# Expert layer: the gathered tokens of a round, from eight column blocks fetched by index and transposed instead of four

## The reference, cut to what matters

```python
e_flat = idx.reshape(-1)                      # 384 tokens x 8 experts
order = jnp.argsort(e_flat)                   # assignments sorted by expert, padded to blocks
x_pad = jnp.concatenate([xt, jnp.zeros((1, D), xt.dtype)], axis=0)
def block(args):
    rows, e = args
    xb = x_pad[rows]                          # the gather
    return (jax.nn.silu(xb @ w1[e]) * (xb @ w3[e])) @ w2[e]
out = lax.map(block, (row_token.reshape(n_blocks, MOE_BLOCK), block_expert)).reshape(R, D)
return jax.ops.segment_sum(out * row_gate[:, None], row_token, num_segments=T + 1)[:T]
```

## Time and profile before

| what | value |
|---|---|
| median of 3 runs | 1431.32 us (1430.42 to 1434.19) |
| the profiled execution's own time | 1430.79 us |
| its span, first to last instruction | 1428.9 us |
| mean granted TensorE clock | 0.994 |
| TensorE products busy | 1392.2 us, 97% of the span, 8025 instructions |
| VectorE, ScalarE, GpSimd busy | 39%, 30%, 21% |
| DMA | 319.70 MB, 223 GB/s read and written in HBM over the span |
| queue 1 (sync) | 307.25 MB in 98416 packets |
| queue 0 (GpSimd's indirect DMAs) | 8.39 MB in 2560 packets |

### The profile page before, as it was taken

How to read it: one execution, slowest core, us unless ns; L and a number is a source line. 1 busy time by engine, 2 the same in 40 slices (tenths; PEclk the granted TensorE clock), 3 DMA queues, 4 the chain that set the end, 5 groups by cost and what they waited for, 6 DMA issues and landing times.

```text
span 1428.9 us, 21288 instructions
## 1 busy us (share of the span) xinstructions
PE 1392.2 (97%) x8025; PEld 984.6 (69%) x8025; DVE 556.2 (39%) x1136; ACT 430.5 (30%) x1021; POOL 306.9 (21%) x247
## 2 busy tenths in 40 slices
PE   7999999999999999999999998999999999999996
PEld 2695898889888986888988865445544455444552
DVE  3467342885356576433222383111212112221124
ACT  3232212222644362223320422222232223222223
POOL 0430323324055542554141010000000000000001
PEclk9999999999999999999999999999999999999998
DMA  9540423213202539321135344999999999999991
GB/s 370 183 134 6 136 81 118 89 60 118 92 27 89 163 143 351 112 89 60 37 126 171 133 192 176 417 418 417 404 400 407 401 397 400 403 403 400 400 385 45
DMA packets 107379, 319.70 MB, mean 224 GB/s; under 512 B 9777, under 2 KB 69937, under 8 KB 78769
## 3 DMA queue, kind: packets, MB, share of 16 engines
q1 hardware_dynamic: 98416, 307.25, 56.0%
q0 software_dynamic: 2560, 8.39, 1.8%
q10 hardware_dynamic: 6336, 3.15, 0.8%
HBM read 314.83 MB, written 3.93 MB: 223 GB/s over the span
## 4 chain that ended last, share of the span: by engine, by line
PE 94%; DMA 2%; DVE 2%; ACT 1%; issue 0%; POOL 0%; SPq 0%; POOLq 0%; DVEq 0%
PE banks L629 21%; PE banks L596 19%; PE banks L2892 16%; PE banks L2941 8%; PE banks L2801 7%; PE banks L1036 4%; PE banks L2779 4%; PE banks L1182 1%; PE banks L868 1%; DMA ring<-in_ada_w 1%; PE banks L603 1%; PE banks L680 1%; PE banks L748 1%; PE banks L2787 1%; PE banks L2793 1%; PE banks L1241 1%
## 5 line engine op out<-in xcount | busy, mean ns | idle before, releaser
L2892 PE MATMUL banks<-w,xg 128*64 128x512 f32 (+1 forms) x1312 | 235.1, 597 | 0.0
L2892 PEld LDWEIGHTS banks<-w,xg 128*64 128x64 f32 (+1 forms) x1312 | 73.8, 127 | 154.5 <-issue 135.5
L3233 POOL DMA_INDIRECT fetched<-token_rows,row_of_place x32 | 30.4, 951 | 503.5 <-DVE row_of_place L3194 456.5
L629 PE MATMUL banks<-hT,ring 128*128 128x192 f32 x792 | 137.7, 326 | 0.0
L629 PEld LDWEIGHTS banks<-hT,ring 128*128 128x128 f32 x792 | 129.7, 190 | 2.1 <-DMA ring<-in_w_in 0.5
L2941 PE MATMUL banks<-w,hidT 128*64 128x512 f32 (+1 forms) x656 | 123.9, 600 | 0.3 <-ACT hidT L2985 0.3
L2801 PE MATMUL banks<-y,selT 128*128 128x512 f32 x384 | 110.7, 410 | 0.0
L629 PE MATMUL banks<-x,ring 128*128 128x192 f32 x528 | 96.9, 327 | 0.9 <-ACT late L1358 0.9
L629 PE MATMUL banks<-x,combos 128*128 128x192 f32 x528 | 96.6, 326 | 0.0
L3075 DVE SCALAR_TENSOR_TENSOR hid<-banks,gslot,sil 128x256 f32<-128x256 f32 x33 | 15.9, 483 | 201.8 <-ACT sil L2983 191.9
L2801 PEld LDWEIGHTS banks<-y,selT 128*128 128x128 f32 x384 | 66.1, 189 | 35.3 <-issue 26.2
(11 more groups left out here) (484 smaller groups left out, 2058.3 us busy)
## 6 DMA issues: line engine op xcount, KB each, us to landing
w<-in_exp_w SPq DMA_DIRECT2D x198, 1024.0 KB, 10.5
ring<-in_w_in SPq DMA_DIRECT2D x46, 1024.0 KB, 5.3
ring<-in_ada_w SPq DMA_DIRECT2D x24, 1024.0 KB, 7.3
ring<-in_w_branch SPq DMA_DIRECT2D x8, 1024.0 KB, 6.1
ring<-in_w_out SPq DMA_DIRECT2D x4, 1024.0 KB, 6.1
arena<-in_sh_w SPq DMA_DIRECT2D x3, 1024.0 KB, 8.0
x<-in_x_sample SPq DMA_DIRECT2D x4, 512.0 KB, 8.4
arena<-in_t_last_layer SPq DMA_DIRECT2D x1, 1024.0 KB, 8.2
```

The source lines that it names most:

```text
L629: last = mm(out, lhsT=w[:, k, :], rhs=tokens[:, k, :], start=start and k == 0, stop=k == KD // 2 - 1, skip_group_check=not start)
L2892: ins = mm(ps[lo:hi, :], lhsT=xg[:, k, a_ * P + lo:a_ * P + hi], rhs=w13[:, a_, u, :, k, :], start=k == 0, stop=k == KD - 1)
L3233: nc.gpsimd.indirect_dma_start(fetched[:, a_, :], None, rows[:, :], bass.IndirectOffsetOnAxis(ap=row_of_place[:, 2 * a_:2 * a_ + 1], axis= ...
```

## The change

`FROM_ROWS`, the first feature that comes from the table, goes from 512 to 0. So the table `token_rows` and the fetched rows hold all 1024 features (4 KB a row instead of 2 KB), all four jobs of the gather are transposes, and the gather products are left in the first pass alone (`AHEAD`). `fetched` is no longer a tile of its own but the first two thirds of `whole_rows`, which is free once the table is stored. TensorE waits for the fetched rows ahead of job 0, and the six scatter products of the stretch stand behind the four jobs as 1, 2, 2 and 1.

```diff
-FROM_ROWS = D // 2
+FROM_ROWS = 0
@@ expert_tiles
-        sb("fetched", P, 2, D - FROM_ROWS),
         sb("whole_rows", P, NT, D - FROM_ROWS),
@@ experts
-    token_ids, row_of_place, fetched, whole_rows = (tiles[n] for n in ("token_ids", "row_of_place", "fetched", "whole_rows"))
+    token_ids, row_of_place, whole_rows = (tiles[n] for n in ("token_ids", "row_of_place", "whole_rows"))
+    fetched = whole_rows[:, 0:2, :]
@@
+    FOLLOWED_BY = [(6, 7), (7, 9), (9, 11), (11, 12)]
@@ body of tensor_part
                 elif a_:
                     pe.wait_ge(s_sel, q + 2)
-                    for job in GATHERS[0:2]:
-                        gather(job[2], open_bank(job))
-                    scatter(1 - a_, 6, 7)
-                    out = open_bank(GATHERS[2])
                     pe.wait_ge(s_fetched, 32 * q + 32)
-                    turn_rows(2, out)
-                    scatter(1 - a_, 7, 10)
-                    turn_rows(3, open_bank(GATHERS[3]))
+                    for job in GATHERS:
+                        turn_rows(job[2], open_bank(job))
+                        scatter(1 - a_, *FOLLOWED_BY[job[2]])
                     pe.wait_ge(s_gq, q + 2)
                     close_bank(turn(0, open_bank(("S", 0, 0))))
-                if add:
-                    scatter(1 - a_, 10 if a_ else 6, 12)
+                if add and not a_:
+                    scatter(1 - a_, 6, 12)
```

## The result

| | before | after |
|---|---|---|
| median | 1431.3 us (1430.42 to 1434.19) | 1457.5 us (1454.11 to 1462.72, 4 runs) |
| profiled execution, span | 1430.79, 1428.9 us | 1454.11, 1452.3 us |
| mean granted clock | 0.994 | 0.992 |

The ratio is 1.019, with an interval of 1.0174 to 1.0207: the change makes the kernel slower by 26 us, where 81 were forecast. The sign and the range held, the size didn't.

The account below looks back on a forecast made before the run. TensorE was taken to set the pace, with the DMA engines nearly full too. Per gather -1.93 + 4.4 + 2.6 = +5.1 us, x16 = +81 us on 1430.8, gave 1512 us, range 1440 to 1545.

Parts of the forecast that it names:

- saving on TensorE: Gather stretch, first gather product to Y: 5.63 us shrinks to 3.70 with transposes for products, saving 1.93 us per gather.
- usual landing of the second fetch, 2 KB rows: Second fetch, issue to landing: 8.8 us, the median of all landings plus half the 1.6 us between one round's two.
- added by 128 more packets: Fetches on queue 0: 4 KB rows go one per packet, 256 data packets for 128, taking 4.6 us more.
- wait: TensorE ahead of the gather's transposes: rows land at 13.4 us against 8.93 available, about 4.4 us idle per gather.
- clock: TensorE after each wait: granted clock falls to 0.50 for several us, losing 2.6 us per gather (bounds 0 and 3.4).
- 4096 data packets more: Queue 0 over the kernel: the expected rise in data packets if each packet holds one row.
- rival 1: Rows late in each gather but clock kept, since rounds are dense up to the wait: +40 us, 1471 us; chance 0.22.
- the turn and one fit in it: Before Y: one transpose group and one scatter product fit in the 1.03 us until VectorE empties the last group's bank.
- The DMA bound: Each round moves 13.63 MB at 418 GB/s, 32.6 us; with rows in time this holds the kernel at 1425 us.
- The point of decision: Wait for the second fetch: rows within 10.9 us of its issue keep TensorE no slower than it was.
- share clearly under 0.95: DMA share in a round: expected below 0.95 if TensorE is late, 1.0 with 418 GB/s if DMA bounds it.
- Rival 3: An engine takes all its rows of a fetch in one turn, hiding the longer transfer: 1425 us; chance 0.05.

Follow-up runs that it names:

- e1: Kernel after, but table and fetches hold only the upper 512 features (2 KB rows), the lower 512 of gathered tokens stale: 1409.5 us (ratio 0.9861).
- e4: Kernel before, its two jobs of gather products kept, but rows of 4 KB stored and fetched: 1431.1 us (ratio 1.0008).
- e8: Kernel after plus a third indirect fetch, of 2 KB rows from their own table, which nothing reads, awaited with the others: 1517.9 us (ratio 1.0621).
- e2: Kernel after without the indirect fetches; TensorE waits for the stored table instead and transposes wrong rows: 1407.7 us (ratio 0.984).
- e3: Kernel after, full rows still fetched, but transposes read tokens already on chip and the fetch is awaited only in Y's second block: 1423.6 us (ratio 0.9956).

## Why the prediction was right in sign and wrong in size

| per gather, us | predicted | measured |
|---|---|---|
| saving on TensorE | -1.93 | -1.43 |
| time from second issue to need | 8.93 | 9.21 |
| usual landing of the second fetch, 2 KB rows | 8.8 | 8.9 |
| added by 128 more packets | +4.6 | +2.9 |
| wait | 4.4 | 2.73 |
| clock | +2.6 | +0.2 |
| sum | +5.1 | +1.5 |

**The step that failed** is the price of the packets, "128/111 x 4.0 = 4.6 us": the second fetch landed 2.9 us later than before, not 4.6. That one row of 4 KB makes one packet was right; the count of "4096 data packets more" was a slip (128 in each of 16 rounds are the 2048 that came). The rate of the window in the earlier trace rows, 36 ns a packet, was not far off: the 256 data packets of both fetches passed in 8.2 us, 32 ns each (median of the 16 rounds, from the start of the first packet to the end of the last). What the sum missed is that the 128 packets of the kernel before had taken 5.4 us, not 4.6, because the last of them straggled. From 1126 to 1128, behind the window of the earlier trace rows, the last 17 (38 less 21 tiny ones) passed beside 82 packets of queue 1. In `e1`, whose rows are 2 KB too, all 128 (164 less 36) passed within 4 us, 1113.8 to 1117.8, beside 133. The kernel before first:

```profile
DMA packets 120, 0.74 MB, mean 371 GB/s; under 512 B 21, under 2 KB 21, under 8 KB 38
```

```profile
DMA packets 297, 1.61 MB, mean 403 GB/s; under 512 B 36, under 2 KB 36, under 8 KB 164
```

So the usual landing of 8.8 us, from which the sum started, held a straggle that doesn't double with the packets. `e1`, without it (3.9 us for its 128 packets), had its rows after 7.6 us, and against that the kernel after is 4.2 later, near the forecast price. `e4` against the kernel before, the same order of TensorE's work with only the rows longer, is 2.1 later. Why the last packets straggle in the kernel before wasn't tried. With +2.9 the prediction's own sum gives a wait of 2.8 us. (Its 13.4 against 8.93 makes 4.5 and not 4.4, which changes nothing here.)

**The clock term** is the second step that failed, and the larger in us (2.4 of the 3.6 between the two sums). The prediction priced a wait by the idle 2.05 us of the first pass, where small products of the plan stood before it. By that row a wait of 2.8 us would have been charged as well: 16 x (-1.93 + 2.8 + 2.6) = +56, twice what came. In the rounds, waits of 2.3 to 3.1 us left the clock alone in 14 of 15 gathers, as rival 1 argued ("the rounds are dense up to the wait"), so the length of the idle time by itself doesn't tell. At 4.4 us the clock would have fallen, as forecast: e8 shows it from 4.2 us on, though at 1.7 us a gather (1.5 and 0.2) and not 2.6, and the measured prices make that 16 x (-1.43 + 4.4 + 1.7) = +75. Rival 1, with the clock kept, gives 1430.8 + 16 x (-1.43 + 2.73) = 1452 with the measured terms: what happened is nearer to it than to the forecast, and lies in the part of the range that was there for it.

**The saving** was 0.5 us too large. The stretch to Y missed by 0.18, of which the 0.26 us wait for VectorE's last copy is the part that shows: "the turn and one fit in it" left no slack. Another 0.1 lies ahead of the transposes: from H to them it was 8.60 us before and is 8.71 in `e2`. The last 0.2 lies in Y. From its start to H it was 3.49 us before (1133.88 in the earlier trace rows to the start of H in the same timeline of the kernel before):

```profile
1137.37 7.04 PE L2892 MATMUL banks<-w,xg 128*64 128x512 f32 x32
```

and is 3.70 us after (1110.80 to 1114.50). Why the same products take longer there wasn't tried.

**What held.** The DMA bound (rounds of 32.5 us in e3, 420 GB/s) and the 1425 us that it gives for rows in time; GpSimd's longer sums (2.37 us each for 1.27) and the stores, hidden. The point of decision, 10.9 us from the issue of the second fetch, is not contradicted, but no landing tried it closely: 8.5 and 8.7 us gave a faster kernel, 11.8 a slower one. The sign of "share clearly under 0.95" did not come: the share is 0.99 at 404 GB/s, since a wait of 2.7 us leaves the engines little time free.

**The page.** Rival 3 fell: 256 packets carry the 256 rows of 4 KB, and they alternate with those of queue 1. The Trainium skill, "DMA: Bandwidth & Descriptors", section on queues, rings and completion order, names 9 to 17 descriptors as typical of a packet; here the data packets of the profile held one row or two, by the length of the row. Whether the page counts its packets as the profile does, no run here tells.

## What to carry to other kernels

When a fetch is made larger, work out how many packets it becomes and what else is in the engines, not only its bytes; and compare its landing with the first instruction that needs it, which the same change may have moved forward. Try the size just under the one planned: here 7/8 of the columns gives 1421.7 us where all of them give 1457.5. Price a clock that depends on a wait from a run or a row with a wait of that length, and carry both ends of the wait through it.

## What the runs showed of the hardware that was not expected

- Indirect fetches pack two rows of 2, 3, 3.5 and 3.75 KB into a packet (4096, 6144, 7168 and 7680 bytes), but rows of 4 KB go one by one. The Trainium skill, "DMA: Bandwidth & Descriptors", section on SWDGE, HWDGE and iDMA, prefers packets of at most 4096 bytes; three of these kernels ran with larger ones, and their rows landed sooner than those of 4 KB (8.2 to 8.7 us for 11.8).
- In dense rounds, waits of 2.3 to 3.1 us left TensorE at full clock in 14 of 15 cases; the one of 2.75 us that brought 3.41 us at half clock was not the longest. What sets it apart wasn't tried.
- The three longer runs of the kernel after had mean clocks of 0.991, 0.990 and 0.988 for the 0.992 of the profiled one (spans 1454.3, 1457.1 and 1460.9 us), so part of the 3.4 us between the profiled execution and the median may be further low stretches; their traces aren't here.
